# Mixture of experts on one core: the last matrix of each block loaded from GpSimd's queue instead of SP's

## What is computed

```
def hierarchical_moe(h, w_rg, b_rg, w_re, b_re, w1, w3, w2):
    ...
    e_id = g_idx[:, None].astype(jnp.int32) * EXPERTS_PER_GROUP + e_loc.astype(jnp.int32)
    ...
    def expert_block(args):
        xb, e = args
        hid = jax.nn.silu(xb @ w1[e]) * (xb @ w3[e])
        return hid @ w2[e]
    ys = lax.map(expert_block, (xs, blk_expert)).reshape(n_pad, D)
    ys = ys * wpad[:, None].astype(ys.dtype)
    out = jnp.zeros((T + 1, D), ys.dtype).at[tok].add(ys)[:T]
```

## Time and profile before

| | |
|---|---|
| median of three runs | 1654.13 us |
| the profiled execution, its own time | 1657.17 us |
| its span, first to last instruction | 1655.1 us |
| mean granted TensorE clock | 0.963 |
| PE busy | 1462.5 us (88%) |
| DVE, ACT, POOL busy | 882.8, 482.4, 285.6 us |
| moved by DMA | 595.80 MB, mean 360 GB/s |
| chain that ended last | PE 55%, DMA 30%, DVE 11% |

### The profile page before, as it was taken

One profiled execution on the slowest core, in us unless ns is written; L12 is line 12 of the kernel. 1 busy time (PEld: TensorE's weight loads), 2 busy tenths in 40 slices (PEclk: granted clock), 3 DMA queues, 4 the chain that ended last, 5 costly groups with the idle time before them and its releaser, 6 DMA issues.

```text
span 1655.1 us, 25299 instructions
## 1 busy us (share of the span) xinstructions
PE 1462.5 (88%) x9902; PEld 1180.6 (71%) x9902; DVE 882.8 (53%) x2303; ACT 482.4 (29%) x1289; POOL 285.6 (17%) x260
## 2 busy tenths in 40 slices
PE   4999998888888888989789899999999998888887
PEld 3888878788888888879778847888855444444444
DVE  5687766787777777777775636521442111111112
ACT  2052212544444444444444412210311111111111
POOL 0000000335344534444445200000000000000000
PEclk9999999899999998999999999999999999999999
DMA  9554785999999999999999978466578999999997
GB/s 390 232 204 153 304 329 218 374 393 421 421 420 417 421 420 419 411 420 421 421 418 416 380 319 318 187 264 248 201 308 368 431 430 430 431 432 431 431 430 318
DMA packets 57115, 595.80 MB, mean 360 GB/s; under 512 B 6464, under 2 KB 6848, under 8 KB 8000
## 3 DMA queue, kind: packets, MB, share of 16 engines
q1 hardware_dynamic: 20160, 326.12, 47.5%
q0 software_dynamic: 36864, 268.45, 39.3%
HBM read 593.50 MB, written 1.05 MB: 359 GB/s over the span
## 4 chain that ended last, share of the span: by engine, by line
PE 55%; DMA 30%; DVE 11%; issue 2%; ACT 1%; POOL 0%; SPq 0%; DVEq 0%; POOLq 0%
PE bank L651 16%; DMA weight_slabs<-in_w_moe 15%; PE bank L913 14%; DMA gathered_rows<-in_expert_uv,work 11%; PE bank L1074 5%; PE bank L818 3%; PE bank L958 3%; PE bank L1047 2%; DMA weight_slabs<-in_slabs 2%; PE bank L1102 1%; DVE gathered_rows L1863 1%; PE bank L847 1%; DVE weight_slabs L1863 1%; DVE weight_slabs L1464 1%; DMA weight_slabs<-in_expert_uv,work 1%
## 5 line engine op out<-in xcount | busy, mean ns | idle before, releaser
L913 PE MATMUL bank<-work,weight_slabs 128*128 128x128 f32 x2048 | 273.8, 297 | 67.2 <-ACT work L1315 67.1
L913 PEld LDWEIGHTS bank<-work,weight_slabs 128*128 128x128 f32 x2048 | 268.0, 212 | 76.8 <-ACT work L1315 74.0
L913 PE MATMUL bank<-work,gathered_rows 128*128 128x128 f32 x2048 | 247.9, 278 | 13.6 <-ACT work L1315 13.5
L913 PEld LDWEIGHTS bank<-work,gathered_rows 128*128 128x128 f32 x2048 | 240.4, 193 | 24.7 <-ACT work L1315 21.9
L1863 DVE CUSTOM_DVE_ANT_0 gathered_rows<-gathered_rows,work 128x1024 f32<-128x1024 f32 x128 | 156.2, 1225 | 131.5 <-DMA gathered_rows<-in_expert_uv,work 130.4
L1398 POOL DMA_INDIRECT gathered_rows<-in_expert_uv,work x128 | 140.7, 1099 | 425.9 <-DVE work L1834 288.0
L651 PE MATMUL bank<-hT,weight_slabs 128*128 128x256 f32 x960 | 212.9, 382 | 1.1 <-ACT hT L1156 1.1
L651 PEld LDWEIGHTS bank<-hT,weight_slabs 128*128 128x128 f32 x960 | 182.9, 191 | 30.2 <-issue 5.4
L1398 POOL DMA_INDIRECT weight_slabs<-in_expert_uv,work x128 | 144.7, 1131 | 220.3 <-PE bank L913 215.3
L1863 DVE CUSTOM_DVE_ANT_0 weight_slabs<-weight_slabs,work 128x1024 f32<-128x1024 f32 x128 | 151.3, 1221 | 35.7 <-DMA weight_slabs<-in_expert_uv,work 32.5
L2060 DVE COPY work<-bank 128x512 f32<-128x512 f32 x32 | 22.1, 691 | 257.3 <-PE bank L1035 257.3
(11 more groups left out here) (345 smaller groups left out, 1632.9 us busy)
## 6 DMA issues: line engine op xcount, KB each, us to landing
weight_slabs<-in_w_moe SPq DMA_DIRECT2D x29, 4096.0 KB, 25.3
weight_slabs<-in_slabs SPq DMA_DIRECT2D x55, 2048.0 KB, 11.7
weight_slabs<-in_w_moe SPq DMA_DIRECT2D x35, 2048.0 KB, 25.4
gathered_rows<-in_w_moe SPq DMA_DIRECT2D x2, 2048.0 KB, 15.0
weight_slabs<-in_slabs SPq DMA_DIRECT2D x2, 1024.0 KB, 14.6
gathered_rows<-in_expert_uv,work POOLq DMA_INDIRECT x128
weight_slabs<-in_expert_uv,work POOLq DMA_INDIRECT x128
weight_slabs<-in_slabs SPq DMA_DIRECT2D x1, 1664.0 KB, 28.6
```

The lines of the kernel that those rows point to most:

```text
L913: ins = nc.tensor.matmul(ps[2 * t + c // 4][:, (c % 4) * P:(c % 4 + 1) * P], row_at[k][:, D + c * P:D + (c + 1) * P], diag[:, k, :], start ...
```

## The change

GpSimd issues the w2 loads of the blocks from 3 on; SP issues only w1 and w3. GpSimd waits on the same values of `m_w2` as SP did, and reads the table of experts itself. Its loads raise two semaphores of their own, one for slot `m2` and one for `m5`, and TensorE's wait ahead of L1102 goes by them in those blocks. The loads of blocks 0 to 2, the sizes, the slots and all arithmetic are as before.

```
-    block_value.append([loads_of_slot[m0] + 16, loads_of_slot[m1], loads_of_slot[m2] + 16])
+    block_value.append([loads_of_slot[m0] + 16, loads_of_slot[m1], 16])
+    second_loaded = {m2: sem("second_a_loaded"), m5: sem("second_b_loaded")}
...
-        def load_second(src, slot):
-
-            sp.dma_start(slabs[:, slot, :], src).then_inc(slab_loaded[slot], 16)
-
...
         load_first(g["w13_moe"][3], m0)
-        sp.wait_ge(m_w2, 2)
-        load_second(g["w2_moe"][3], m2)
...
                 load_first(g["w13_moe"][bass.ds(e, 1)].rearrange("o p n -> p (o n)"), BLOCK_SLOTS[4 + par][0])
-                sp.wait_ge(m_w2, (i * 2 + par - 1) * 2)
-                load_second(g["w2_moe"][bass.ds(e, 1)].rearrange("o p n -> p (o n)"), BLOCK_SLOTS[4 + par][2])
...
-            pe.wait_ge(slab_loaded[s2], v2)
+            pe.wait_ge(second_loaded[s2] if late else slab_loaded[s2], v2)
...
+        def load_second(src, slot):
+
+            nc.gpsimd.dma_start(slabs[:, slot, :], src).then_inc(second_loaded[slot], 16)
+
+        for e, done_blocks, slot in ((3, 1, m2), (4, 2, m5), (5, 4, m2)):
+            pool.wait_ge(m_w2, 2 * done_blocks)
+            load_second(g["w2_moe"][e], slot)
+        pool.wait_ge(table_ready, 1)
+        npair = pool.value_load(npair_sb[0:1, :], min_val=NEXP // 2, max_val=(NEXP + OVER) // 2)
+        with pool.Fori(3, npair) as i:
+            for par in range(2):
+                e = pool.value_load(etab[0:1, bass.ds(i * 2 + par, 1)], min_val=0, max_val=NEXP - 1)
+                pool.wait_ge(m_w2, (i * 2 + par - 1) * 2)
+                load_second(g["w2_moe"][bass.ds(e, 1)].rearrange("o p n -> p (o n)"), BLOCK_SLOTS[4 + par][2])
```

More of the change, by code:

```diff
@@ L593, in _ @@
         load_first(g["w13_moe"][3], m0)
-        sp.wait_ge(m_w2, 2)
-        load_second(g["w2_moe"][3], m2)
         sp.wait_ge(m_w13, 2)
         load_first(g["w13_moe"][4], m3)
-        sp.wait_ge(m_w2, 4)
-        load_second(g["w2_moe"][4], m5)
         sp.wait_ge(m_w13, 4)
         load_first(g["w13_moe"][5], m0)
-        sp.wait_ge(m_w2, 8)
-        load_second(g["w2_moe"][5], m2)
         sp.wait_ge(table_ready, 1)
@@ L1056, in _, with expert_block @@
         wait_emptied(pe, "cnt")
-        def expert_block(n1, par, slots, values, first=False, ahead=False):
+        def expert_block(n1, par, slots, values, first=False, ahead=False, late=False):
             s1, s3, s2 = slots
@@ L1106, in _ @@
         for b in range(4):
-            expert_block(b + 1, b % 2, BLOCK_SLOTS[b], block_value[b], first=b == 0)
+            expert_block(b + 1, b % 2, BLOCK_SLOTS[b], block_value[b], first=b == 0, late=b == 3)
         pe.wait_ge(table_ready, 1)
@@ L1112, in _ @@
                 slots = BLOCK_SLOTS[4 + par]
-                expert_block(i * 2 + (par + 1), par, slots, [i * 16 + (pair_base[slots[0]] - 16), loads_of_slot[slots[1]], i * 16 + (pair_base[slots[2]] - 16)], ahead=True)
+                expert_block(i * 2 + (par + 1), par, slots, [i * 16 + (pair_base[slots[0]] - 16), loads_of_slot[slots[1]], i * 16 if par else i * 16 - 16], ahead=True, late=True)
         pe.wait_ge(placeT_out, npair * 2 + 1)
```

## The result

The kernel with the split loads takes 1659.41 us (median of 22 runs, 1653.7 to 1667.14), the kernel before 1654.9 us (22 runs): a ratio of 1.0024, 95% interval 1.0015 to 1.0032, or 4.0 us (2.5 to 5.3). The ratio is worked out from all the runs; the two medians differ by 4.5 us. The forecast was a shift of 2.4 us, 1656.5 on the median then known, in a range of 1653 to 1667. The profiled execution took 1659.47 us with a span of 1657.7.

A forecast was written before the change was run, and what follows sets the result against it. The prediction took bytes moved, up to the landing of the last w1 and w3, as the bound. Nothing saved on issue, the last block starting 4.87 - 2.4 = 2.4 us later: 1654.13 + 2.4 = 1656.5 us, range 1653 to 1667.

The forecast's parts named there:

- The bound, and Y: Experts' part: bytes moved at 431 GB/s, 14.61 us a block, bound it; the end of the stream of loads doesn't move.
- No wait of SP's to save: term 0: SP's w13 loads don't stand behind its wait for w2, so none is issued earlier; saving 0.
- One packet of each queue in turn: Engines alternate between SP's 32 KB and GpSimd's 16 KB rows: w13 gets two thirds of the time, w2 one third.
- burst: Rival: an engine takes all eight rows of a load before it turns, w2 passing w13 whole; 1659 to 1662 us, chance 0.13.
- The arrears, and 2.4 us at the end: w2 falls 0.56 us behind for six or seven blocks; four of eight packets remain, so block 31 starts 2.4 us later.
- The landing of w13 is its last row: Block 31: start shift counted only w2 rows left when w13 lands, 4.87 - 2.4 = 2.4 us.
- The starts of the queues: Replay's time from issue to data: 1.5 us for SP, 2.3 for GpSimd; varying GpSimd's from 1.0 to 4 gives 3.0 to 1.8.
- GpSimd's and VectorE's part: 0: One w2 load instruction a block on GpSimd, 0.5 us between it and VectorE, leaves the replay at 2.4 us; cost taken as 0.
- Same, within 0.3%: Whole kernel: the 2.4 us shift is under the 0.3% (5.0 us) a measurement can tell, so it counts as the same; chance 0.56.
- w2 starves: Rival: GpSimd's packets under 16 KB give w2 less than a third, with waits at L1102; +11.7 us, 1665.8, chance 0.17.
- A slower queue: Rival: GpSimd's queue itself is slower, a w2 packet costing 0.62 to 0.65 us; +4.7 to +10.8 us, 1659 to 1665, chance 0.10.
- no change of order: Rival: engines finish w13 first, or the change doesn't reach the order of service; 1654.1 us, chance 0.05.

The follow-up runs named there:

- last-two-blocks kernel: Against the changed kernel, SP instead of GpSimd loads w2 of blocks 30 and 31, behind their w13; 1656.65 us, ratio 1.0015 (1.0001 to 1.003).

## Why the prediction was right, and where it was not

*The bound, and Y.* Right. Y, the end of the loads, stands 383.2 and 383.4 us behind the copy of block 4 before, 383.4 and 383.3 with the change. 430 GB/s and 14.60 to 14.61 us a block on either side, and filling 7.1 us of idle DMA time early shortened the stretch by 6.7.

*No wait of SP's to save: term 0.* Right. SP's w13 loads are issued as late as before, 3.84 us into a block. In the last-two-blocks kernel SP has both loads and both waits again, and its stretch is 3.0 us shorter.

*One packet of each queue in turn.* Right, and the step on which all rests. 93.88 MB against 47.99 MB, packets of 16 KB, w2 landing after 25.5 us (23 to 27 forecast). In the packet records from 1400 to 1640 us, a packet begins within 0.02 us of the end of another, 16 side by side; in 4637 of these 4736 steps the queue changes. The three kernels with other row sizes moved the share as turns by rows say, if not always by the expected amount. At the end four rows of w2 are left and not none, and the burst's landing under 8 us never appeared.

*The arrears, and 2.4 us at the end.* Right to the row: the first wait came at block 10 (11 or 10 forecast), and four of eight rows are left.

*The landing of w13 is its last row.* Here the sum was short. It left out the packet that raises the semaphore, which takes a turn of its own: one w2 row, 0.61 us. So the last block starts 3.05 us later and not 2.4. The measured 3.0 and 3.2 us lie on either side of it, by the 0.1 and 0.2 us by which Y differs between executions.

*The starts of the queues.* The replay took 2.3 us for GpSimd and 1.5 for SP. The GpSimd load issued at 1250.18 has no packet in the DMA view until 1252.5 and two by 1253: 2.3 to 2.8 us. SP's of 1244.25 has none until 1244.8 and six by 1245.3: 0.6 to 1.1 us. The difference was larger than assumed, about 1.7 instead of 0.8, read from one load of each; it stayed without effect, since the forecast depends on it little (1.8 to 3.0 us for 1.0 to 4).

*GpSimd's and VectorE's part: 0.* Right: 0.53 us an issue, with no one behind it, and ScalarE's queue gives the same loss.

*Same, within 0.3%.* Right, at 0.24% with an interval from 0.15 to 0.32%, so nearer to the border than 2.4 us would be. The interval leaves out 1: it is a real loss, though a small one. The ratio's 4.0 us are 0.8 more than the stretch shows, within their own interval of 2.5 to 5.3 us. The median of 1659.41 us lies just above the forecast's own range of 1655.3 to 1659 and inside the wide one of 1653 to 1667. That one also had room for w2 starving and for the burst, so the time alone would not have told them apart; the waits, the landings and the stretch do.

*The rivals.* w2 starves: not here, but at 8 KB rows it came as worked out, +10.8 us for +11.7 by the stretch, 7.9 by the ratio. A slower queue: no, 430 GB/s. Burst, no change of order, faster: none seen.

## What to carry to other kernels

In this stretch, bound by bytes at 430 GB/s, a second queue brought nothing by itself: it changed the order of service, row by row in turn, so each queue's share went by the size of its rows (66.1 to 34.2% at 32 and 16 KB). Ask which load ends the stretch and what may stand behind it: with one queue the whole last w2, 4.89 us, stood behind the last w13, with two only 2.44 us of it. The gain, 6.7 us of the stretch, lay where the DMA engines had been idle before: look in the windows for a gap, and for memory that is free at that moment.

## What the runs showed of the hardware

- Loads of two queues took turns row by row. From 1400 to 1640 us the queue changed in 4637 of 4736 steps from one packet to the next in the changed kernel (SP's rows of 32 KB, GpSimd's of 16), in 4642 of 4725 with ScalarE's queue in GpSimd's place, and in 9074 of 9343 with both in half rows, of 16 and 8 KB. With 32 and 8 KB the loads landed 16.3 and 23.3 us after issue, with 16 and 16 KB 21.5 and 14.0 us, against 25.3 and 25.5 us in the changed kernel. In the changed kernel and in that with ScalarE's queue the sum stayed at 430 and 431 GB/s.
- Each load had 16 packets of 4 bytes, one for each count of its semaphore: 541 and 541 from 1400 to 1640 us in the changed kernel. They took turns too: the last one of w13 came 0.01 us behind its last row with one queue, 0.61 to 0.63 us with GpSimd's full of 16 KB rows, 0.61 to 0.62 with ScalarE's, and at most 0.32 with GpSimd's full of 8 KB rows.
- Rows of 32 KB were cheaper than smaller ones: a block took 14.61 us in the kernel before, 14.69 with w13 in 16 KB rows from one queue, 14.76 with w2 in 8 KB rows from GpSimd's queue as well. The smaller rows came with more loads, but the rows show it themselves: from 1400 to 1600 us a row of 32 KB took 1.217 us of an engine and one of 16 KB 0.615 in the kernel before, and one of 8 KB 0.312 in the one with both in half rows.
- One plain load from GpSimd, issued at 1250.18 in the changed kernel, took 2.3 to 2.8 us from its issue to its first packet; one from SP, issued at 1244.25 in the kernel before, 0.6 to 1.1 us.
- The wait for the last stores was 1.8 us in one execution of the kernel before and 3.9 us in the other.
